# A hybrid retention and sliding-window encoder in fp32: the first head of the first block computed by plain products, and its weight sums made elsewhere

## The reference

```
h = x @ w_in;  q, k (4 heads x 256),  v, g (4 heads x 512) = split(h)
q, k = rope(q), rope(k) / 16
att   = (q k^T) * decay mask              # within a chunk
r     = att v + (q state) * xi            # state: 256 x 512 per head, carried over the tokens
state = state * decay + (k * zeta)^T v
x = post_norm(x, (silu(g) * groupnorm(r)) @ w_out)
```

## Time and profile before

| | |
|---|---|
| median of 3 runs | 2439.64 us (2438.74 to 2440.88) |
| the profiled execution | 2436.53 us |
| its span in the profile | 2434.6 us |
| PE busy | 96% of the span |
| DVE busy | 74% |
| ACT busy | 49% |
| POOL busy | 14% |
| matmul records | 11506 |

### The profile page before, as it was taken

The page is one execution under the profiler, slowest core; times in us unless marked ns, Lnnn a source line. Parts: engine busy times, 40 slices in busy tenths (PEclk is TensorE's granted clock), DMA queues, the critical chain, the costliest instruction groups (busy, mean ns, idle before and its releaser), DMA issues.

```text
span 2434.6 us, 30987 instructions
## 1 busy us (share of the span) xinstructions
PE 2327.5 (96%) x11506; PEld 1892.1 (78%) x11506; DVE 1812.7 (74%) x2577; ACT 1181.6 (49%) x1753; POOL 343.8 (14%) x350
## 2 busy tenths in 40 slices
PE   6889999989999999999999999999999999999996
PEld 5777777867778888887777888888777888888775
DVE  6877888855986678884697766886479667787458
ACT  3433445346544445535744544553664445554463
POOL 4212201102001110111211011110121110011031
PEclk9999999999999999999999999999999999999998
DMA  9787677671664445755275544585247345454413
GB/s 332 278 303 255 220 242 237 231 264 55 209 225 154 127 133 173 243 167 171 72 254 177 167 150 131 167 272 185 80 146 268 113 139 165 122 186 151 139 62 121
DMA packets 215061, 443.38 MB, mean 182 GB/s; under 512 B 15040, under 2 KB 52432, under 8 KB 211328
## 3 DMA queue, kind: packets, MB, share of 16 engines
q1 hardware_dynamic: 200832, 375.58, 47.8%
q0 software_dynamic: 14080, 65.83, 7.3%
HBM read 379.75 MB, written 57.41 MB: 180 GB/s over the span
## 4 chain that ended last, share of the span: by engine, by line
PE 64%; DVE 19%; DMA 7%; issue 5%; ACT 4%; SPq 1%; POOL 0%; DVEq 0%; ACTq 0%; POOLq 0%
PE accs L655 18%; PE accs L656 17%; PE accs L657 17%; DVE w_lo L1274 6%; DMA stage<-t_prep 5%; ACT w_hi L964 2%; PE bank L655 2%; PE bank L656 2%; PE bank L657 2%; PE bank L882 2%; DMA stage<-swa_w_in 1%; PE bank L891 1%; PE bank L901 1%; PE bank L746 1%; DVE ra L1308 1%
## 5 line engine op out<-in xcount | busy, mean ns | idle before, releaser
L1274 DVE TENSOR_TENSOR w_lo<-stage,w_hi 128x1024 fp32r<-128x1024 f32 x536 | 668.4, 1253 | 396.6 <-ACT w_hi L964 395.5
L964 ACT ACTIVATE w_hi<-stage 128x1024 fp32r<-128x1024 f32 x536 | 563.6, 1056 | 554.7 <-DMA stage<-t_prep 243.6
L655 PE MATMUL accs<-w_hi,xs 128*128 128x512 f32 x1120 | 448.5, 400 | 40.8 <-ACT sg L969 15.7
L657 PE MATMUL accs<-w_hi,xs 128*128 128x512 f32 x1120 | 441.4, 394 | 0.0
L656 PE MATMUL accs<-w_lo,xs 128*128 128x512 f32 x1120 | 440.7, 393 | 0.0
L655 PEld LDWEIGHTS accs<-w_hi,xs 128*128 128x128 f32 x1120 | 212.9, 190 | 94.4 <-issue 42.2
L655 PE MATMUL accs<-x_hi,w_hi 128*128 128x512 f32 (+1 forms) x640 | 246.6, 385 | 11.8 <-DVE qT L1763 10.7
L657 PEld LDWEIGHTS accs<-w_hi,xs 128*128 128x128 f32 x1120 | 212.9, 190 | 45.8
L1885 POOL TENSOR_TENSOR rstd<-ve,half 128x1 f32<-128x1 f32 x96 | 82.4, 858 | 1175.8 <-DVE ve L1330 1133.2
L656 PEld LDWEIGHTS accs<-w_lo,xs 128*128 128x128 f32 x1120 | 213.1, 190 | 42.2
L656 PE MATMUL accs<-x_lo,w_hi 128*128 128x512 f32 (+1 forms) x640 | 238.1, 372 | 0.0
(11 more groups left out here) (184 smaller groups left out, 3861.6 us busy)
## 6 DMA issues: line engine op xcount, KB each, us to landing
stage<-t_prep SPq DMA_DIRECT2D x224, 512.0 KB, 4.7
stage<-ret_w_in SPq DMA_DIRECT2D x96, 512.0 KB, 4.2
stage<-ret_w_in SPq DMA_DIRECT2D x128, 256.0 KB, 3.1
stage<-swa_w_in SPq DMA_DIRECT2D x64, 512.0 KB, 4.2
t_prep<-t_buf POOLq DMA_DIRECT2D x28, 1024.0 KB, 6.2
stage<-ret_w_out SPq DMA_DIRECT2D x48, 512.0 KB, 3.7
cs<-rope_t SPq DMA_DIRECT2D x16, 1024.0 KB, 7.1
t_buf<-ret_w_in POOLq DMA_DIRECT2D x32, 512.0 KB, 9.7
```

What stands on the lines that cost most here:

```text
L655: mm(dst, lhs[0], rhs[0], start=start, stop=False, skip_group_check=reopened)
L657: return mm(dst, lhs[1], rhs[0], start=False, stop=stop, skip_group_check=reopened)
L964: copy(w_hi[:, g % HS], stage[:, g % LS], ACT.Copy).then_inc(w_hi_made, 1)
L1274: nc.vector.tensor_tensor(w_lo[:, g % LS], stage[:, g % LS], w_hi[:, g % HS].bitcast(F32), sub).then_inc(w_split, 1)
```

## The change

The first head of block 0 computes v and gate by plain products: eight weight pairs (slots 4 to 11, four for v and four for the gate) of 24 matmuls each, all four banks at once, in place of fourteen pairs of 12 matmuls. Slots 12 to 17 of block 0 are vacant: nothing is loaded, split or multiplied there; the engines still walk through them for their other work. Weight sets 0 to 3 are first used in block 1. They are loaded in slots 105 to 109 and made in slots 107 to 113 of block 0; sets 2 and 3 have new buffers for it (4 and 5, in the space `QR` and `ST`). The start loads sets 4 to 7 in their place, and sets 4 to 23 have other slots and buffers. The retention steps of the first head stand behind slots 8, 9 and 10, its first score behind slot 6. A cache of ready-made weights, empty before, is removed with its branches.

```diff
+PLAIN = range(VG, VG + 8)
+VACANT = range(VG + 8, HEAD)
...
+def plain(s, p):
+
+    return s == 0 and p in PLAIN
...
-T_PLAN = [(0, 0, -1, 1), (1, 1, -1, 1), (2, 2, -1, 2), (3, 3, -1, 2), (4, 0, 8, 11), (5, 1, 9, 13), (6, 2, 10, 14),
...
+T_PLAN = [(4, 0, -1, 3), (5, 1, -1, 3), (6, 2, -1, 4), (7, 3, -1, 5), (8, 0, 4, 6), (9, 1, 5, 12), (10, 0, 8, 18),
...
+    return VG + 2 if H == 0 else VG + 5
...
+    return (VG + 4, VG + 5, VG + 6) if H == 0 else (VG + 7, VG + 10, VG + 13)
...
@@ SP: load_pair
-                if g >= NS * NP or ready_made(g):
+                if g >= NS * NP or vacant(g):
                     return
                 s, p = divmod(g, NP)
                 need(sp, products, used(g - LS))
...
@@ PE
+            def plain_vg_pair(p):
+
+                j, i = divmod(p - VG, 4)
+                wait_weights(p)
+                for m in range(4):
+                    if i == 0:
+                        fill = VG + (4 * j if m < 2 else 2 + 4 * j)
+                        need(pe, acc_free[m], prior(0, fill, m))
+                    for u in range(2):
+                        k = 2 * i + u
+                        phys = m // 2 if k < 4 else (2, 6)[m // 2]
+                        cols = slice(m % 2 * P, (m % 2 + 1) * P)
+                        mm = mm3(acc[m], (xs[:, phys, 0, k % 4, cols], xs[:, phys, 1, k % 4, cols]), weights(p, u),
+                                 k == 0, k == KD - 1)
+                    if m == 1:
+                        mm.then_inc(products, 1)
+                mm.then_inc(products, 1 if p < PLAIN[-1] else 1 + 2 * len(VACANT))
...
@@ ACT
+                        if v == 4 and H == 0:
+                            act.wait_ge(xs_split, 4)
+                            act.wait_ge(products, used(VG + 2) + 1)
+                            copy(v_hi[:, 0:2, :], accs[:, 0:2, :], ACT.Copy).then_inc(v_hi_made, 1)
+                            act.wait_ge(products, used(VG + 3))
+                            copy(v_hi[:, 2:4, :], accs[:, 2:4, :], ACT.Copy).then_inc(v_hi_made, 1)
...
+                            if v == 8:
+                                act.wait_ge(bias_copied, 1)
+                                act.wait_ge(products, used(VG + 6) + 1)
+                                copy(sg[:, 0:2, :], accs[:, 0:2, :], ACT.Silu).then_inc(x_free, 6)
+                                act.wait_ge(products, used(VG + 7))
+                                copy(sg[:, 2:4, :], accs[:, 2:4, :], ACT.Silu).then_inc(y_free, 4)
...
@@ DVE
+                        if H == 0 and v == 4:
+                            nc.vector.tensor_tensor(v_lo[:, 0:2, :], accs[:, 0:2, :], v_hi[:, 0:2, :].bitcast(F32),
+                                                    sub).then_inc(x_free, 2)
+                            dve.wait_ge(v_hi_made, 2)
+                            nc.vector.tensor_tensor(v_lo[:, 2:4, :], accs[:, 2:4, :], v_hi[:, 2:4, :].bitcast(F32),
+                                                    sub).then_inc(y_free, 2)
...
@@ POOL: load_t
+                if b >= 4:
+                    wait_sums_stored(pool, 1)
+                elif n >= SO_SET:
```

More of the change, by code:

```diff
@@ L379, in last_set, with weight_pair @@
         def last_set(b):
-            return max(n for n in range(SO_SET) if T_BUF[n] == b)
-        def wait_kept(eng, g):
-            if to_keep(g):
-                eng.wait_ge(w_kept[g % LS], KEEPS[g])
+            return [n for n, buf, _, made in T_PLAN if buf == b and made < RO][-1]
         def set_of(kind, h):
             return {"vg": 4 * h, "ro": RO_SET, "so": SO_SET}[kind]
-        def weight_pair(p, part):
+        def weight_pair(s, p, part):
+            if plain(s, p):
+                j, i = divmod(p - VG, 4)
+                return w_vg[:, i // 2, 2 * (i % 2):2 * (i % 2) + 2, j, 0, :]
             kind, c, q, i = PAIRS[p]
@@ L492, in load_pair @@
                 need(sp, products, used(g - LS))
-                wait_kept(sp, g - LS)
                 kind, c, q, i = PAIRS[p]
-                if s == 0 and q in T_INDEX:
+                first_use = s == (1 if (kind, c) == ("vg", 0) else 0)
+                if first_use and q in T_INDEX:
                     for n in range(set_of(kind, c) + 2 * i, set_of(kind, c) + 2 * i + 2):
@@ L843, in retain @@
                 if t == 0:
-                    pe.wait_ge(v01_split, H + 1)
+                    if H == 0:
+                        pe.wait_ge(x_free, emptied(0, VG, 1))
+                    else:
+                        pe.wait_ge(v01_split, H)
                     pe.wait_ge(q_split, H + 1)
@@ L848, in retain @@
                     s, h = divmod(H, RH)
-                    pe.wait_ge(x_free, emptied(s, first_pair("vg", h, "P4"), 1))
+                    if H == 0:
+                        pe.wait_ge(y_free, emptied(0, VG + 2, 3))
+                    else:
+                        pe.wait_ge(x_free, emptied(s, first_pair("vg", h, "P4"), 1))
                 pe.wait_ge(ret_ready, n + 1)
@@ L918, in _ @@
                         continue
-                    if kind in ("vg", "ro", "so"):
+                    if plain(s, p):
+                        plain_vg_pair(p)
+                    elif vacant(s * NP + p):
+                        continue
+                    elif kind in ("vg", "ro", "so"):
                         strassen_pair(s, p)
@@ L1887, in gate @@
             def gate(H, t):
-                pool.wait_ge(gate_made, 2 * (H + 1))
+                if H == 0:
+                    pool.wait_ge(x_free, emptied(0, first_pair("vg", 0, "P4"), 1))
+                    pool.wait_ge(y_free, emptied(0, first_pair("vg", 0, "P3"), 3))
+                else:
+                    pool.wait_ge(gate_made, 2 * H)
                 pool.wait_ge(r_normed, 4 * H + t + 1)
@@ L1918, in _ @@
                 pool.wait_ge(x_loaded[w], 16)
-            for n in range(4):
-                load_t(n)
+            for n, _, at_slot, _ in T_PLAN:
+                if at_slot < 0:
+                    load_t(n)
             pool.wait_ge(init_done, 3)
```

127 lines of the change are left out of this document (54 added, 73 removed), and 8 rows, old and new, of the table T_PLAN.

## The result

The changed kernel takes 2451.49 us as the median of five runs (2448.34 to 2454.82), the kernel before 2438.88 (2432.62 to 2440.88) in the same measurement: a ratio of 1.0054, 95% interval [1.0042, 1.0066], or +13.2 us of 2438.9. The forecast was -3.0. The profiled execution has a span of 2446.3 us.

A forecast was written before the change was run, and what follows sets the result against it. Block 0's early stages were taken to lose time to TensorE waits and slow-clock restarts. The terms +9.0 - 6 - 3.5 - 4 + 1.5 gave -3.0 us, from a median of 2439.6 to 2436.6 us; range 2427 to 2447.

The forecast's parts named there:

- First head, +9.0: Block 0's first head: 24 more matmuls, new TensorE waits and slow restarts cost +9.0 us, between +5 and +13.
- The four waits: TensorE in the first head waits for Y banks 4.4, rotated q 0.8, v's residual 4.8, next head's weights 6.9 us.
- Second head, -6: Block 0's second head: two set loads and the bias-table spread come after the crowded stretch, -6 us, bounds 0 and 7.7.
- Third q,k stage, -3.5: q,k stage ahead of the third head: ACT's buffer gets its last set a slot earlier, -3.5 us, bounds 0 and 4.3.
- third head, -4: Block 0's third head: the set made in its middle moves ahead of it, -4 us, bounds 0 and 7.1.
- Fourth head and RO stage, 0: Fourth head keeps its number of sets within a slot or two: 0, within 2 us; output projection had no term.
- Slots 104 to 114, +1.5: End of block 0: sets 0 to 3 expose only the move of keys and values, +1.5 us, bounds 0 and +6.
- DVE half idle hides it: Slots 104 to 114: DMA engines 25% busy and DVE half idle behind the jam hide nearly all the new sets' cost.
- The upper bound of +6: Slots 104 to 114: highest cost allowed for the moved sets, +6 us where +1.5 was taken.
- the rival on taking turns: At the jam, POOL's new loads slow key/value moves and next weights: +6 for +1.5, 2441 us; chance 0.14.
- the relief does not come: Second and third heads: set loads fall beside the same loads, 3 us of relief, +7.5 in all, 2447 us; chance 0.22.

The follow-up runs named there:

- e2: Changed kernel with v's copies and low part put ahead of pair 11's weight parts in slot 8; 2441.37 us, 1.0018 of the kernel before.
- e1: Changed kernel with loads and high parts behind the vacant slots waiting for their buffer's last real user, pair 18's high part made earlier; 2445.75 us, 1.0029 of the kernel before.
- e3: Changed kernel with the load of weight set 16 asked for at slot 31 in place of 28; 2452.18 us, 1.0057 of the kernel before.
- e5: Changed kernel with sets 8 to 23 loaded and made in the slots of the kernel before; 2448.20 us, 1.0040 of the kernel before.
- e9: The mixed plan: changed kernel with e1's and e2's edits, sets 13 to 23 near their slots of before; 2431.73 us, 0.9973 of the kernel before.
- e12: Changed kernel with e9's slots for sets 8 to 23 alone, without the first head's edits; 2448.30 us, 1.0026 of the kernel before.
- e4: Changed kernel without making sets 0 to 3, leaving out part of the computation; 2447.80 us, 1.0038 of the kernel before.
- e7: Changed kernel with sets 0 to 3 loaded at slots 106 to 110 and made at 109 to 114; 2451.19 us, 1.0054 of the kernel before.
- e14: e9 with other buffers for sets 15 to 21, freeing those ACT writes turned results over earlier; 2434.56 us, 0.9986 of the kernel before.
- e6: Changed kernel with the edits of e1 and e2 together; 2437.09 us, 1.0000 of the kernel before.
- e10: e9 with sets 0 to 3 loaded at slots 108 to 112 and made at 111 to 116; 2435.25 us, 0.9992 of the kernel before.
- e13: e6 with sets 13, 18 and 22 made one slot after the score slots, loads of 16, 20, 23 later; 2433.51 us, 0.9971 of the kernel before.

## Why the prediction was wrong

**First head, +9.0: right in kind, near in size.** The four waits were forecast as 4.4, 0.8, 4.8 and 6.9 and measured 5.46, 0.70, 4.83 and 6.09 us, the second q,k stage was to begin at 115.6 and began at 114.37, and the second v,gate stage begins 7.55 us later than before. The load behind the vacant slots landed 3.3 us after its issue, where 4.0 was taken. The Trainium skill (DMA: Bandwidth & Descriptors, Anatomy of one DMA) gives the formula that I quoted beside this term for transfers that GpSimd issues, and this load is SP's; the sum did not use it. Taking away the wait for v (e2) was worth 8.8 us where wait and restart had been counted as 6.3, and the one for pair 18 (e1) 6.1 for 8.4.

**Second head, -6, measured +3.1. This step failed.** (The stage takes 62.5 to 63.1 us in the three profiles of this order, 59.4 before.) It said that two set loads and the spread would leave the crowded stretch, and it misread that stretch: POOL issued two set loads there, not three (137.22 and 139.73). Both are gone from it, but the loads of sets 14 and 15 stand at 146.20 and 158.22 in the changed kernel, and the spread at 179.82, still in the second head. POOL's queue moved 7.2 MB in this stage before and 6.2 MB now. The plan moves the makes of sets 4 to 23 by 0 to 11 slots, not by 1 to 15. So little left: the DMA share of 140 to 160 us went from 0.98 to 0.89. The low-part waits of PE, has one, are gone, but others came, since I did not price what the moved entries stand in front of: set 16's load ahead of the root on POOL, set 13's make (2.8 us) in the score's slot on DVE. e3 removed the first alone, and a wait of the same size for a load came in its place. Other slots (e5, e9, e12) bring the stage back to 58 or 60 us.

**Third q,k stage, -3.5, measured -1.4, and third head, -4, measured 0. These steps failed too.** With the same order, e4 and e7 show +0.1 for the q,k stage, so hardly anything came. The buffer's last set was made one slot earlier, no more; e14 shows that the whole 4.2 us can be had there, and that the heads beside it then take it back. Behind that lies a count that I did not make: slots 22 to 57 held the makes of ten sets (12 to 21) before and nine after. In the third head the transfers did become fewer, 13.4 MB for 16.2, and it took as long as before: there a wait of 2.65 us for `att_lo` is new, behind the make of set 18 in the score's slot. The mixed plan moves 15.1 MB in that stage and takes 53.8 us. So it is not the megabytes that set this stage's length.

**Fourth head and RO stage, 0, measured -1.2 and +4.8.** The RO stage was in no term. It takes 91.8 to 95.6 us in the seven profiles with the changed slots of sets 22 and 23 (changed, e1 to e4, e6, e7) and 89.9 to 91.9 in the eight with other slots for them.

**Slots 104 to 114, +1.5, measured +5.7 from k and v to the second block.** The profiles with the same order from there on range from +1.5 (e9) to this +5.7, and the timed runs without the sets say some 4 us. "DVE half idle hides it" was the failing step: a set's make waits on DVE for a load that the jam delays, 8.5 us, and the softmax waits behind it. The upper bound of +6 and the rival on taking turns had this size. The Trainium skill (DMA: Bandwidth & Descriptors, Queues, rings and completion order) says that a DMA engine takes turns between the queues that have work; the trace of e10 agrees, where SP issued the carried values at 503.1, ahead of POOL's set loads at 506.1 and 510.9, and they still took 19.6 us for the mixed plan's 10.9. The changed kernel's own transfer shows nothing of it, as e4 tells.

The rival "the relief does not come" had the mechanism, a set load on POOL that waits for its buffer's store, but kept a relief of 3 us; its +7.5, 4.2 more for the jam and the RO stage's 4.8, which no case had, come to 16.5 for the 18.5 of the profile at the second block. That sum is of one profile, and part of it is luck: behind the second block the same profile got 6 us back, and the timed result is +13.2. Two of the rivals came together, and they had been priced as alternatives. The range ended 4.5 us below the result.

What stays open: why the second v,gate stage and the third q,k stage hold 10 to 19 us more than undisturbed ones (78.7 us) in every profile, how the 7.1 us of e13 divide, and what the better slots would bring to the kernel before: no run has them without the changed first head.

## What to carry to other kernels

Before an entry in an in-order list is moved, name what stands behind it on that engine in the new place, its load and its store as well as its arithmetic; a slot that is free on average may be the one between a score and its low part. A slot number is a time only for an engine that waits for something in that slot: to delay a transfer, give it a wait, not a number. And count what a stretch still holds after the move: relief is priced by the waits that hang on the work that leaves it, and a wait taken away there is real only if the next stage does not take it back.

## What the runs showed that I had not expected

Three set makes shifted by one slot, with three loads, were worth 7 us, as much as the change of the first head's algorithm. The changed kernel comes out ahead only with both repairs and other slots: -0.27% [0.14, 0.40] in e9, -0.29% [0.17, 0.41] in e13. How much of that is the algorithm's and how much the slots' is not shown.
